# A two-layer decoder with routed experts: down units singly and in pairs among the column units, and the next rows turned in the H banks

## What is computed

```python
def expert_block(args):
    xb, e = args                                  # up to 128 rows of 1024, expert e
    return (silu(xb @ w_gate[e]) * (xb @ w_up[e])) @ w_down[e]
```

## Time and profile before

| | |
|---|---|
| median of three runs | 1443.62 us |
| the profiled execution | 1442.83 us |
| its span, first to last instruction | 1441.2 us |
| TensorE busy | 1401.6 us, 97% |
| VectorE busy | 1184.1 us, 82% |
| ScalarE busy | 976.8 us, 68% |
| read from HBM | 438.90 MB |
| seven rounds | 597.1 to 1389.0 us of the span |

### The profile page before, as it was taken

The page is one execution under the profiler, slowest core; times in us unless marked ns, Lnnn a source line. Parts: engine busy times, 40 slices in busy tenths (PEclk is TensorE's granted clock), DMA queues, the critical chain, the costliest instruction groups (busy, mean ns, idle before and its releaser), DMA issues.

```text
span 1441.2 us, 19684 instructions
## 1 busy us (share of the span) xinstructions
PE 1401.6 (97%) x7106; PEld 1211.1 (84%) x7106; DVE 1184.1 (82%) x1183; ACT 976.8 (68%) x975; POOL 164.1 (11%) x206
## 2 busy tenths in 40 slices
PE   8989999999999999999999999999999999999997
PEld 6758888888988888988888798888888978888976
DVE  7866545545886679899989988889999899999997
ACT  7565434445524486787778777788788778878775
POOL 1000200000333069100100010020020010010002
PEclk9999999999999999999999999999999999999999
DMA  9525885554633469999999999999999999999994
GB/s 337 193 76 187 311 308 197 183 180 134 205 119 105 153 194 404 360 420 398 402 415 388 374 415 369 352 391 413 378 418 410 384 386 421 390 419 408 368 417 176
DMA packets 101919, 452.51 MB, mean 314 GB/s; under 512 B 10026, under 2 KB 19330, under 8 KB 87488
## 3 DMA queue, kind: packets, MB, share of 16 engines
q1 hardware_dynamic: 94496, 433.09, 78.5%
q0 software_dynamic: 5456, 17.06, 3.2%
q10 hardware_dynamic: 1872, 1.12, 0.3%
HBM read 438.90 MB, written 14.17 MB: 314 GB/s over the span
## 4 chain that ended last, share of the span: by engine, by line
PE 75%; DVE 10%; issue 5%; ACT 3%; DMA 1%; DVEq 0%; ACTq 0%
PE bank L1977 23%; PE bank L1979 23%; PE bank L1978 22%; DVE w_lo L1322 4%; DVE wide_lo L1322 2%; PE bank L2190 1%; DVE work L1858 1%; ACT wide_hi L883 1%; PE bank L2366 1%; ACT w_hi L883 1%; DMA raw<-in_w_up_moe_dram 1%; PE bank L1983 1%; PE bank L1984 1%; ACT work L1162 1%; DVE w_lo L1332 1%
## 5 line engine op out<-in xcount | busy, mean ns | idle before, releaser
L1322 DVE TENSOR_TENSOR w_lo<-raw,w_hi 128x1792 fp32r<-128x1792 f32 (+1 forms) x269 | 561.5, 2113 | 33.0 <-ACT w_hi L883 29.5
L883 ACT ACTIVATE w_hi<-raw 128x1792 fp32r<-128x1792 f32 (+1 forms) x269 | 476.1, 1781 | 104.6 <-PE bank L1979 90.4
L1977 PE MATMUL bank<-w_hi,t_hi 128*128 128x448 f32 (+2 forms) x1016 | 385.9, 380 | 5.4 <-DVE w_lo L1322 2.5
L1978 PE MATMUL bank<-w_lo,t_hi 128*128 128x448 f32 (+2 forms) x1016 | 379.3, 373 | 0.0
L894 ACT ACTIVATE w_hi<-raw 128x1024 fp32r<-128x1024 f32 (+1 forms) x99 | 102.3, 1033 | 212.0 <-PE bank L1979 208.2
L1977 PEld LDWEIGHTS bank<-w_hi,t_hi 128*128 128x128 f32 x1016 | 191.1, 188 | 35.1 <-issue 4.2
L1979 PE MATMUL bank<-w_hi,t_hi 128*128 128x448 f32 x600 | 219.3, 365 | 0.0
L1327 DVE TENSOR_TENSOR w_lo<-raw,w_hi 128x1024 fp32r<-128x1024 f32 (+1 forms) x99 | 122.5, 1237 | 112.3 <-ACT w_hi L894 112.1
L1978 PEld LDWEIGHTS bank<-w_lo,t_hi 128*128 128x128 f32 x1016 | 191.0, 188 | 24.4 <-issue 1.0
L1322 DVE TENSOR_TENSOR wide_lo<-raw,wide_hi 128x1792 fp32r<-128x1792 f32 (+1 forms) x75 | 156.0, 2080 | 38.2 <-ACT wide_hi L883 38.0
L1979 PE MATMUL bank<-w_hi,t_lo 128*128 128x512 f32 (+2 forms) x464 | 177.9, 384 | 0.0
(11 more groups left out here) (404 smaller groups left out, 1947.3 us busy)
## 6 DMA issues: line engine op xcount, KB each, us to landing
raw<-in_w_gate_moe_dram SPq DMA_DIRECT2D x128, 896.0 KB, 8.3
raw<-in_w_up_moe_dram SPq DMA_DIRECT2D x128, 896.0 KB, 8.0
raw<-in_w_down_moe_dram SPq DMA_DIRECT2D x112, 1024.0 KB, 8.6
raw<-in_w_in_rec_dram SPq DMA_DIRECT2D x16, 1024.0 KB, 5.5
raw<-in_w_gate_dense_dram SPq DMA_DIRECT2D x14, 1024.0 KB, 5.1
raw<-in_w_up_dense_dram SPq DMA_DIRECT2D x14, 1024.0 KB, 5.1
raw<-in_w_down_dense_dram SPq DMA_DIRECT2D x14, 1024.0 KB, 5.1
raw<-in_w_in_attn_dram SPq DMA_DIRECT2D x8, 1024.0 KB, 15.3
```

The source lines that it names most:

```text
L883: act.activation(hi_of[slot_at_unit(u - 1)][:, 0:width], raw[:, r, 0:width], ACT.Copy).then_inc(hi_done, 1)
L1322: dve.tensor_tensor(lo_of[s][:, 0:width], raw[:, r, 0:width], hi_of[s][:, 0:width].bitcast(F32), ALU.subtract).then_inc(lo_done, 1)
L1977: pe.matmul(o, lh, rh, start=start, stop=False)
L1978: pe.matmul(o, lh, rl, start=False, stop=False)
```

## The change

The table `PLAN` gets another order. Gate part 0 is now four units, d0, four units, d1 and d2; up part 0 is three, d3, three, d4, two, d5 and d6; gate part 1 as part 0 with d7, then d8 and d9; up part 1 as part 0 with d10, d11, then d12 and d13. Before, eight column units stood together, with four, four, two and four down units behind them. The places of the H turns and the hidden splits move with it. The rows of the expert after next are turned at place 42, into the H banks, in place of 44 into banks 1 and 3; ScalarE copies them when the last up unit (place 43) is done, VectorE subtracts behind the lo of place 45, and empties the up banks after that and after the lo of the next round's first unit.

```diff
-PLAN = (column_units("gate", 0) + down_units_of(0, 4) + ...
+GATE_PIECES, UP_PIECES = ((4, 1), (4, 2)), ((3, 1), (3, 1), (2, 2))
+PLAN = (spaced("gate", 0, GATE_PIECES, 0) + spaced("up", 0, UP_PIECES, 3)
+        + spaced("gate", 1, GATE_PIECES, 7) + spaced("up", 1, UP_PIECES, 10))
...
-TRANSPOSE_AT = {2: 0, 3: 1, 6: 2, 7: 3, 15: 4, 17: 5, 27: 6}
-HIDDEN_AT = (2, 3, past("down", 0, 1), ...
+TRANSPOSE_AT = {1: 0, 2: 1, 5: 2, 7: 3, 15: 4, 19: 5, 26: 6}
+HIDDEN_AT = (1, 2, past("down", 0, 1), ...
-ROWS_AT = past("down", 0, 11)
+ROWS_AT, LAST_FIRST_AT = past("down", 0, 11), past("up", 1)
+def later_transposes(g):
+    return sum(h > g and h % 2 == g % 2 and p <= before_down(2 * g) for p, h in TRANSPOSE_AT.items())
...
 # ScalarE, end of a round
-                split_to(start + ROWS_AT + 2)
...
-                    gather_hi(t_hi)
+                    split_to(start + LAST_FIRST_AT + 2)
+                    act.wait_ge(unit_done, unit_at(start + LAST_FIRST_AT))
+                    gather_hi(t_hi, (TR, TR + 1))
...
 # VectorE, end of a round
-                up_rows(1, start + past("up", 1), order=(1, 3, 0, 2))
-                split_to(start + ROWS_AT + 2)
...
-                    gather_lo(t_hi)
+                    split_to(start + LAST_FIRST_AT + 2)
+                    gather_lo(t_hi, (TR, TR + 1))
+                    up_rows(1, start + past("up", 1))
...
 # TensorE, down_unit: the wait for the H bank
-                    later = 0 if into or g + 2 >= FB else 1
-                    pe.wait_ge(free[TR + hp], n.at(f"fill{TR + hp}", later))
+                    pe.wait_ge(free[TR + hp], n.at(f"fill{TR + hp}", 0 if into else later_transposes(g)))
...
 # TensorE, phase
                     elif p == ROWS_AT:
-                        row_transposes()
+                        row_transposes((TR, TR + 1))
```

More of the change, by code:

```diff
@@ L95, with column_units, spaced @@
 FIRST_GATHER = (6, 7)
-def column_units(name, part):
-    return [(name, part, k) for k in range(KC)]
+def column_units(name, part, first=0, count=KC):
+    return [(name, part, k) for k in range(first, first + count)]
 def down_units_of(first, count):
     return [("down", 0, j) for j in range(first, first + count)]
-PLAN = (column_units("gate", 0) + down_units_of(0, 4) + column_units("up", 0) + down_units_of(4, 4)
-        + column_units("gate", 1) + down_units_of(8, 2) + column_units("up", 1) + down_units_of(10, 4))
+def spaced(name, part, pieces, first):
+    plan, k = [], 0
+    for columns, downs in pieces:
+        plan += column_units(name, part, k, columns) + down_units_of(first, downs)
+        k, first = k + columns, first + downs
+    return plan
+GATE_PIECES, UP_PIECES = ((4, 1), (4, 2)), ((3, 1), (3, 1), (2, 2))
+PLAN = (spaced("gate", 0, GATE_PIECES, 0) + spaced("up", 0, UP_PIECES, 3)
+        + spaced("gate", 1, GATE_PIECES, 7) + spaced("up", 1, UP_PIECES, 10))
 FIRST_PLAN = [u for part in range(PARTS) for name in ("gate", "up") for u in column_units(name, part)]
@@ L115, in past, with before_down @@
     return PLAN.index((name, part, k)) + 1
-TRANSPOSE_AT = {2: 0, 3: 1, 6: 2, 7: 3, 15: 4, 17: 5, 27: 6}
-HIDDEN_AT = (2, 3, past("down", 0, 1), past("down", 0, 3), past("down", 0, 5), past("down", 0, 7),
+def before_down(j):
+    return PLAN.index(("down", 0, j))
+TRANSPOSE_AT = {1: 0, 2: 1, 5: 2, 7: 3, 15: 4, 19: 5, 26: 6}
+HIDDEN_AT = (1, 2, past("down", 0, 1), past("down", 0, 3), past("down", 0, 5), past("down", 0, 7),
              past("down", 0, 9))
-ROWS_AT = past("down", 0, 11)
+ROWS_AT, LAST_FIRST_AT = past("down", 0, 11), past("up", 1)
+def later_transposes(g):
+    return sum(h > g and h % 2 == g % 2 and p <= before_down(2 * g) for p, h in TRANSPOSE_AT.items())
 TABLE_AT, FIRST_ROWS_AT = 18, 28
@@ L1145, in _, with gather_hi @@
                                    scale=col[:, 24 + k:25 + k]).then_inc(th_done, 1)
-            def gather_hi(rows_t):
-                for m, b in enumerate((GATE + 1, UP + 1)):
+            def gather_hi(rows_t, banks):
+                for m, b in enumerate(banks):
                     wait_full(b)
@@ L1195, in phase @@
                 hidden(6, small)
-                split_to(start + ROWS_AT + 2)
                 if last:
[L1198 to L1201, removed]
+                    split_to(start + ROWS_AT + SPL)
+                    wait_full(TR)
+                    act.activation(ST[:], bank[TR][:, 0:TOK], ACT.Copy).then_inc(free[TR], 1)
+                    split_to(start + LAST_FIRST_AT + SPL)
+                    act.wait_ge(unit_done, unit_at(start + LAST_FIRST_AT))
                     hidden_hi(1)
                 else:
-                    gather_hi(t_hi)
+                    split_to(start + LAST_FIRST_AT + 2)
+                    act.wait_ge(unit_done, unit_at(start + LAST_FIRST_AT))
+                    gather_hi(t_hi, (TR, TR + 1))
                 split_to(start + ROUND_UNITS + AHEAD)
@@ L1218, in _ @@
             split_to(U0 + FIRST_ROWS_AT + 2)
-            gather_hi(t_lo)
+            gather_hi(t_lo, (GATE + 1, UP + 1))
             split_to(start + AHEAD)
@@ L1831, in _, with gather_lo @@
                 ins.then_inc(free[b], 1)
-            def gather_lo(rows_t):
-                for m, b in enumerate((GATE + 1, UP + 1)):
+            def gather_lo(rows_t, banks):
+                for m, b in enumerate(banks):
                     wait_full(b)
@@ L1877, in phase @@
                     hidden(g, small)
-                up_rows(1, start + past("up", 1), order=(1, 3, 0, 2))
-                split_to(start + ROWS_AT + 2)
                 if last:
-                    saw(GATE + 1)
-                    split_to(start + ROUND_UNITS - 2 + SPL)
+                    split_to(start + ROWS_AT + SPL)
+                    saw(TR)
+                    up_rows(1, start + past("up", 1))
                     hidden_lo(1)
                 else:
-                    gather_lo(t_hi)
+                    split_to(start + LAST_FIRST_AT + 2)
+                    gather_lo(t_hi, (TR, TR + 1))
+                    up_rows(1, start + past("up", 1))
                 split_to(start + ROUND_UNITS + AHEAD)
@@ L1892, in _ @@
             split_to(U0 + FIRST_ROWS_AT + 2)
-            gather_lo(t_lo)
+            gather_lo(t_lo, (GATE + 1, UP + 1))
             up_rows(1, U0 + GU, UB)
@@ L2484, in gather, with row_transposes @@
                     last.then_inc(full[b], 1)
-            def row_transposes():
+            def row_transposes(banks):
                 pe.wait_ge(row_block, n.step("row", 16))
-                for m, b in enumerate((GATE + 1, UP + 1)):
+                for m, b in enumerate(banks):
                     open_bank(b)
@@ L2496, in _, with phase @@
             gather()
-            def phase(small_down, small_next, rows_t, last=False):
+            def phase(small_down, small_next, rows_t, last=False, rows_in=(TR, TR + 1)):
                 before = n.count["u"]
@@ L2502, in phase @@
                     if p == 0:
-                        drained(GATE + 1, UP + 1)
+                        drained(*rows_in)
                     if p in TRANSPOSE_AT:
@@ L2507, in phase @@
                         pe.wait_ge(last_done, TT)
-                        open_bank(GATE + 1)
+                        open_bank(TR)
                         for t in range(TT):
-                            one_hot = pe.transpose(bank[GATE + 1][:, t * P:(t + 1) * P], SL[:, t, :], ident[:])
-                        one_hot.then_inc(full[GATE + 1], 1)
+                            one_hot = pe.transpose(bank[TR][:, t * P:(t + 1) * P], SL[:, t, :], ident[:])
+                        one_hot.then_inc(full[TR], 1)
                         expert_transposes(0, into=1)
                     elif p == ROWS_AT:
-                        row_transposes()
+                        row_transposes((TR, TR + 1))
                     if name == "down":
@@ L2533, in _ @@
                 if p == FIRST_ROWS_AT:
-                    row_transposes()
+                    row_transposes((GATE + 1, UP + 1))
                 if p in (0, KC // 2):
@@ L2537, in _ @@
                 expert_unit(k, GB if name == "gate" else UB, t_hi, False)
[L2538 removed]
+            phase(False, True, t_lo, rows_in=(GATE + 1, UP + 1))
             phase(True, False, t_hi)
```

4 lines of the change are left out of this document (2 added, 2 removed).

## The result

The changed kernel takes 1457.05 us (median of four runs, 1455.92 to 1457.78), the kernel before in the same runs 1443.30 (1442.76 to 1443.74). The ratio is 1.0095, with a 95% interval of 1.0077 to 1.0112. The forecast was 1448.3 with a range up to 1453.0, so the time lies outside. Slower was right, and the number is that of the third rival, 1457, which had a chance of 0.08.

A forecast was written before the change was run, and what follows sets the result against it. It took TensorE's work plus waits as the bound, VectorE and DMA within a few per cent. Waits going from 30.6 to 35.3 us add 4.7 to 1442.83: 1447.5, or 1448.3 on the median; range 1441.5 to 1453.

The forecast's parts named there:

- the third rival: TensorE's granted clock falls behind each of six d12 waits: 9 us on top, 1457; chance 0.08.
- the clock falls behind the new wait: Same as the third rival: 1.5 us lost at 0.62 mean clock behind each of six d12 waits; chance 0.08.
- The difference of the two walks: TensorE's waits worked out by arithmetic for old and new order: 30.6 to 35.3 us, 4.7 us slower.
- d12: Round's end: TensorE waits for the gathered rows' subtraction, 2.9 us in rounds 2, 3, 5; 3.6 in 1, 4, 6.
- Removed at the round's end and in the middle: Packed-down rounds: 0.5 + 1.15 + 1.0 inside and 1.3 behind go; d3 and d7 lose 2.6, 0.2 left. Packed-up: 0.6.
- d0: Middle of packed-down rounds: at place 4, waits 1.0 us for a small expert's hidden block.
- Middle of packed-up rounds: Packed units by threes: waits 0.6 (d3), 0.55 (d4), 0.6 (d10), 0.4 (d11), replacing some 3.5 us.
- the old walk: Arithmetic for the order before: 30.6 us of TensorE waits, 4.0 in round 4 and 4.9 in round 6.
- The first H turn of round 1: Now behind one gate unit, it waits 2.0 us until VectorE's first `up_rows` empties bank 4.
- The last expert's first unit: Behind round 7: waits 2.6 us for `up_rows` and its hidden split; with 0.5 at d13, equals the old loss, 3.2.
- The d12 wait is not there: Rival: the wait at d12 is absent or covered, waits return behind the round; some 1440 us; chance 0.12.
- DMA is the bound: Rival: DMA engines, busy 1.00 in six rounds, set the time and hide all of it; 1443.6 us; chance 0.12.

The follow-up runs named there:

- e5: Changed kernel with 13 small matmuls that add zero, ahead of d12 in rounds 1 to 6: 1449.62 us, ratio 1.0054.
- e1: Changed kernel, but d12 no longer counts the row turn into bank 4: 1442.09 us, ratio 0.9995.
- e3: e1, with VectorE emptying banks 4 and 5 one lo earlier ahead of round 1: 1440.65 us, ratio 0.9983.
- e7: e3, with d0 and d7 one place later and the last expert's first hidden split between two pairs of `up_rows`: 1435.10 us, ratio 0.9946.
- e2: Changed kernel with 26 small matmuls that add zero, ahead of d12 in rounds 1 to 6: 1465.09 us, ratio 1.0152.
- e6: Changed kernel with 6 small matmuls that add zero, ahead of d12 in rounds 1 to 6: 1454.16 us, ratio 1.0063 to 1.0091 by interval.
- e8: Changed kernel's order, but rows turned in banks 1 and 3 at place 45, behind `up_rows` of those banks: 1439.78 us, ratio 0.9983.

## Why the prediction was wrong

**The step that failed** is the rival "the clock falls behind the new wait". Its mechanism, its place and its size were written down (1.5 us behind each of six waits, 9 in all; measured 1.6 and 9.4), but it had a chance of 0.08, nothing of it stood in the sum, and the range ended 4 us short of it. The reason given was that the earlier trace rows show a clock of 1.00 with idle times up to 1.10, and that "waits of 2.9 to 3.6 have no row". That is no reason to put the term at nothing: the idle 1.10 us are further from 2.9 than the window from 72 us, where TensorE idles 1.8 of four, and behind that window stands 0.62. Taken from that row alone, the term is 9 and the forecast 1457. But the rows did not settle it that way either. The longest idle time of the kernel before among the experts' units, ahead of round 1, left the matmuls at 0.36 and 0.37 us and the clock at 1.00:

```profile
551.22 0.47 PE L1977 MATMUL bank<-w_hi,t_hi 128*128 128x448 f32 x1 [1.72 <-DVE w_lo L1327]
```

And the fall of the earlier trace rows does not come each time: in the profile of the changed kernel the same place, as idle as before, has none:

```profile
72.00:76.00 4.00, 2.17 (x18) 1.41 (x18) 3.19 (x21) 3.23 (x12) 1.23 (x7) 1.00 0.71 260
76.00:80.00 4.00, 3.41 (x24) 2.14 (x21) 1.95 (x11) 2.11 (x8) 0.00 (x0) 1.00 0.00 0
```

So what the rows allowed was a weighed term and a range that reaches 1457, not a term of nothing. The Trainium skill, "TensorE: Matmul & The Clock Gate", Part 1, said that an idle engine is put back to half rate; the trace agrees at each of the six d12 waits, with 0.50 in the row from 705.5, and does not at the last expert's first unit, where the matmuls behind 2.75 idle us last 0.39.

**The difference of the two walks was right.** e5, the changed kernel without the clock's falls at d12, is the test. Against the kernel before, its rounds stand as follows, and beside them what the prediction gave as the difference of waits:

| round | 1 | 2 | 3 | 4 | 5 | 6 | 7 and the unit behind |
|---|---|---|---|---|---|---|---|
| predicted | +4.2 | -1.2 | +1.6 | +1.8 | -1.2 | +0.9 | -1.4 |
| measured | +4.3 | -1.4 | +1.7 | +1.8 | -0.8 | +0.9 | -3.8 in the round |

For the unit behind round 7 the stretch from there to the end gives +2.5 in the changed kernel, so -1.3 in the last column. The sum is +5.2 for +4.7.

**Term by term.**
- d12: waits of 2.9 and 3.6 with restart were forecast. TensorE sat idle 2.6 in rounds 2, 3 and 5 and 3.4 in rounds 1, 4 and 6: with the 0.35 of a restart 2.9 and 3.7. The prediction names no row for the 0.35; around 1.65 idle us of e1 (at 1164.28) the starts lie 2.04 and then 0.28 apart, in place of 0.23 and 0.20, so a restart costs some 0.24 beyond the idle time, and the waits come to 2.8 and 3.6. Released by `gather_lo` six times, and not in round 7, as said. The bounds of 1.5 to 4.2 were not needed.
- Removed at the round's end and in the middle: no wait of TensorE at the row turn is left among its waits, nor at d3 and d7 of packed-down rounds. d0 waits up to 0.8 there, 1.1 with restart (1.0 forecast).
- Middle of packed-up rounds: four waits of 0.4 to 0.6 were forecast, and one is there, 0.2 to 0.4 idle. In the kernel before, rounds 4 and 6 have three of some 0.3 idle where the old walk has 4.0 and 4.9 us in all. Both walks are too high here by about as much, and that this falls out of their difference is luck.
- The first H turn of round 1: 2.0 forecast, 2.0 measured. The last expert's first unit: 2.6 forecast, 2.75 idle.
- Not foreseen in any term: these two waits can bring a half clock as well, some 1.6 us at the first H turn in e1, some 2.9 at the last expert in e3.

**The rivals.** "The d12 wait is not there" was taken as 1440; e1 makes it so and gives 1442.1 in the median; its profiled execution, 1440.95, holds a half clock of some 1.6 us at the first H turn. "DMA is the bound" is out: e7 reads the same 438.90 MB at 1435 us, and its packed-down rounds move 408 to 412 GB/s where the earlier trace rows have 395 to 399. The same bytes in a shorter round: the DMA engines did not set the length of the round before. (The prediction's 352 to 421 GB/s leave out the last slice of the earlier trace rows, 176; nothing hangs on it.)

## What to carry to other kernels

A wait of TensorE can have two prices: its own length, and the matmuls behind it at half clock, here 1.6 us for each fall at d12. In these profiles the second price came behind 15 of 22 waits of 2.0 us or more and behind one of 21 shorter ones (counted below). So a reordering that gathers short waits into a few long ones can lose more than the sum of its waits says, and a forecast should carry that term with a weight of its own. Look for the second price in the granted clock of a narrow window behind the wait (a window over a round shows 0.99) and in the length of the matmuls, not in the busy share, which stayed at 97%. And when one bank gets a second user, look at every count that waits for that bank: here one number in one wait stood between 13.75 us lost and a kernel as fast as before.

## What was not expected of the hardware

Whether the clock falls behind an idle time is not settled by its length. Counted from the idle times of 1.1 us and more between matmuls of the expert stage (from 590 us on), in the profiles of all eleven kernels: of 13 idle times of 2.6 to 3.4 us, 11 had a stretch at 0.50 within 4 us; of nine of 2.0 to 2.1 us, four; of 21 of 1.1 to 1.8 us, one. The same idle time of the same instruction had it in one execution and not in the next (2.0 us at the first H turn: in e1 and e2, not in the changed kernel, e5, e6 or e8; 2.75 us at the last expert's first unit: in e2 to e6, not in e1 or the changed kernel). What else decides it stays open.

The spread of repeated times goes with it. Of e3's eleven executions the three with a mean granted clock of 0.997 took 1438.8 to 1439.3 us, the six with 0.996 took 1440.3 to 1441.4, the two with 0.995 took 1442.6; of e7's five, two with 0.999 took 1433.1 and 1433.3, three with 0.997 took 1435.1 to 1435.2. One such stretch, 3.4 us at 0.50 in the row from 705.5, is 0.0012 of the mean clock, and its 1.6 us are 0.1% of the time. Only the profiled execution of each kernel shows where its stretches lie, so a difference of 1 or 2 us between two medians can be a difference in how often the clock fell.

Two more numbers: each of the zero matmuls, 64 columns in float32, stands in the trace as two records 0.11 us apart, so 13 of them are 26 records and 2.9 us; and with these matmuls over a column of zeros in place of the idle time, the granted clock stayed at 1.00 at all six d12 places of e5.
